# The remainders of one weight slot in four move from VectorE to GpSimd

## The reference

```
mod = silu(c) @ w_mod + b_mod                          # 2048 -> 6 x 2048
proj = (rmsnorm(x, pre_mix_g) * (1 + scale_a) + shift_a) @ w_in
q = rmsnorm(q_lat) @ w_uq ;  kv = rmsnorm(kv_lat) @ w_ukv
x = x + gate_a * rmsnorm(concat(attn, hgrn) @ w_out)
x = x + gate_m * rmsnorm(square(relu(h @ w_up)) @ w_down)
proj = rmsnorm(x) @ w_in_2
merged = sigmoid(ga) * (att @ w_attn_o) + sigmoid(gb) * (silu(ln(conv)) @ w_conv_o)
x = x + rmsnorm(merged @ w_out_2)
x = x + rmsnorm((silu(gate) * up) @ w_down_2)
```

## Time and profile before

| | |
|---|---|
| median of 3 runs | 2996.82 us (2993.32 to 3002.66) |
| profiled execution | 2995.96 us, span 2994.2 us |
| TensorE (PE) busy | 2751.9 us, 92% |
| VectorE (DVE) busy | 1968.1 us, 66% |
| ScalarE (ACT) busy | 1201.4 us, 40% |
| GpSimd (POOL) busy | 22.6 us, 1% |
| w_lo, VectorE, full chunks | 852 x 1223 ns |

### The profile page before, as it was taken

How to read it: one execution, slowest core, us unless ns; L and a number is a source line. 1 busy time by engine, 2 the same in 40 slices (tenths; PEclk the granted TensorE clock), 3 DMA queues, 4 the chain that set the end, 5 groups by cost and what they waited for, 6 DMA issues and landing times.

```text
span 2994.2 us, 41611 instructions
## 1 busy us (share of the span) xinstructions
PE 2751.9 (92%) x14939; PEld 2350.7 (79%) x14939; DVE 1968.1 (66%) x2489; ACT 1201.4 (40%) x1521; POOL 22.6 (1%) x42
## 2 busy tenths in 40 slices
PE   2299898699799999999979999999979999999998
PEld 2288797567688888888868878887768888888886
DVE  6899685569888445664464878867565565565444
ACT  2134323334444334444344434454444444444433
POOL 1000000000000000000010000000000000000000
PEclk7599899789899999999989999999989999999999
DMA  9799432329487556665546555555536666656554
GB/s 320 254 366 367 150 113 55 108 77 324 155 282 261 177 189 185 188 184 186 179 131 185 176 171 153 164 163 164 171 96 191 184 183 188 188 182 204 182 184 147
DMA packets 491558, 563.46 MB, mean 188 GB/s; under 512 B 17943, under 2 KB 434131, under 8 KB 491072
## 3 DMA queue, kind: packets, MB, share of 16 engines
q1 hardware_dynamic: 489824, 558.18, 58.4%
q0 software_dynamic: 1632, 3.89, 0.6%
HBM read 559.90 MB, written 2.10 MB: 188 GB/s over the span
## 4 chain that ended last, share of the span: by engine, by line
PE 78%; DVE 10%; DMA 8%; ACT 2%; issue 2%; DVEq 0%; SPq 0%; ACTq 0%
PE ps L653 42%; PE ps L655 21%; DMA w_raw<-in_w_in 5%; PE ps L688 3%; PE ps L689 3%; PE ps L690 3%; DMA w_raw<-in_w_mod 2%; PE ps L843 2%; DVE w_lo L1265 2%; DVE mod_acc L1307 2%; ACT w_hi L996 1%; DVE mod_acc_a L1541 1%; PE ps L793 1%; PE ps L720 1%; DVE rstd L1385 1%
## 5 line engine op out<-in xcount | busy, mean ns | idle before, releaser
L653 PE MATMUL ps<-acts,w_hi 128*128 128x512 f32 x4976 | 1780.8, 402 | 46.0 <-DVE acts L1403 15.5
L1265 DVE TENSOR_TENSOR w_lo<-w_raw,w_hi 128x1024 fp32r<-128x1024 f32 (+1 forms) x872 | 1055.1, 1213 | 737.6 <-ACT w_hi L996 601.3
L655 PE MATMUL ps<-acts,w_lo 128*128 128x256 f32 x4976 | 1400.7, 281 | 0.0
L996 ACT CAST w_hi<-w_raw 128x1024 fp32r<-128x1024 f32 (+1 forms) x784 | 814.5, 1042 | 1198.5 <-PE ps L655 1044.5
L653 PEld LDWEIGHTS ps<-acts,w_hi 128*128 128x128 f32 x4976 | 941.3, 189 | 288.3 <-issue 45.6
L655 PEld LDWEIGHTS ps<-acts,w_lo 128*128 128x128 f32 x4976 | 946.5, 190 | 2.1 <-issue 1.7
L653 PE MATMUL ps<-ff,w_hi 128*128 128x512 f32 x1024 | 361.7, 397 | 0.0
L655 PE MATMUL ps<-ff,w_lo 128*128 128x256 f32 x1024 | 288.4, 282 | 0.0
L653 PEld LDWEIGHTS ps<-ff,w_hi 128*128 128x128 f32 x1024 | 193.4, 189 | 45.5
L1307 DVE SCALAR_TENSOR_TENSOR mod_acc<-mod_w,silu_c,mod_acc 128x512 f32<-128x512 f32 (+1 forms) x300 | 192.8, 643 | 9.4 <-DVE mod_acc L1307 0.6
L655 PEld LDWEIGHTS ps<-ff,w_lo 128*128 128x128 f32 x1024 | 193.9, 189 | 0.1
(11 more groups left out here) (244 smaller groups left out, 1612.8 us busy)
## 6 DMA issues: line engine op xcount, KB each, us to landing
w_raw<-in_w_in SPq DMA_DIRECT2D x236, 512.0 KB, 4.4
w_raw<-in_w_down SPq DMA_DIRECT2D x216, 512.0 KB, 3.5
w_raw<-in_w_gate_up SPq DMA_DIRECT2D x176, 512.0 KB, 3.6
mod_w<-in_w_mod SPq DMA_DIRECT2D x128, 512.0 KB, 8.3
w_raw<-in_w_up SPq DMA_DIRECT2D x128, 512.0 KB, 4.1
w_raw<-in_w_mod SPq DMA_DIRECT2D x64, 512.0 KB, 5.2
w_raw<-in_w_out SPq DMA_DIRECT2D x64, 512.0 KB, 4.8
w_raw<-in_w_attn_o SPq DMA_DIRECT2D x16, 512.0 KB, 3.4
```

What stands on the lines that cost most here:

```text
L653: pe.matmul(ps[:, bank, :], hi, lin_.act[:, kk, :, :], start=at_first, stop=False, skip_group_check=True)
L655: mm = pe.matmul(ps[:, bank, 0:T], lo, lin_.act[:, kk, 0, :], start=False, stop=at_last, skip_group_check=True)
L996: act.copy(w_hi[:, slot, 0:kn, 0:lin_.width], w_raw[:, slot, 0:kn, 0:lin_.width]).then_inc(hi_ready, 1)
L1265: dve.tensor_tensor(low[cut], raw[cut], high[cut].bitcast(F32), ALU.subtract).then_inc(lo_ready, 1)
```

## The change

GpSimd computes the remainder of the chunks in slot 3, VectorE those of slots 0 to 2. `lo_ready` becomes four counters, one per slot, and `lo_uses` gives the count that a chunk's remainder brings its slot to. SP and TensorE wait for the counter of the chunk's own slot. VectorE no longer waits for `hi_ready` of slot 3 and goes on to what stands beside the chunk. GpSimd's remainders stand in its queue around the DMAs it already issued.

```diff
-        lo_ready = sem("lo_ready")
+        lo_ready = [sem(f"lo_ready{s}") for s in range(SLOTS)]
...
+        def lo_uses(ph, it, j):
+            return ph.use0[j % SLOTS] + it * ph.slot_uses[j % SLOTS] + (j // SLOTS + 1 - DT)
...
-                    sp.wait_ge(lo_ready, free)
+                    sp.wait_ge(lo_ready[j % SLOTS], lo_uses(ph, it, j) - 1)
...
+            def remainders(ph, it):
+                slot = SLOTS - 1
+                for j in range(slot, ph.n_chunks, SLOTS):
+                    b, _, kn = ph.chunks[j]
+                    lin_ = ph.body[b][0]
+                    cut = (slice(None), slot, slice(0, kn), slice(0, lin_.width))
+                    raw, high, low = wide if lin_.by_token else (w_raw, w_hi, w_lo)
+                    pool.wait_ge(hi_ready, chunk_seq(ph, it, j) + 1)
+                    pool.tensor_tensor(low[cut], raw[cut], high[cut].bitcast(F32),
+                                       ALU.subtract).then_inc(lo_ready[slot], 1)
...
+            remainders_of(("in_h", "in_m"))
             pool.wait_ge(h_lo, 1)
             pool.dma_start(pos_i[ROPE:P, :],
...
+            remainders_of(("uq", "ukv", "w_o", "up_0", "down_0", "up_1", "down_1"))
             pool.wait_ge(*r_m1.added(4))
...
                     pool.dma_start(bias[rows, r // 2, :, i, :], src).then_inc(bias_landed, 16)
+            remainders_of(("in_c", "in_qk", "in_v", "in_g", "att_o", "conv_o", "out_2", "gate_up"))
             pool.wait_ge(extra, extra_all("gate_up"))
             pool.dma_start(g_row[:, :], ...
+            remainders_of(("down_2",))
...
-                    pe.wait_ge(lo_ready, chunk_seq(ph, it, j) + 1)
+                    pe.wait_ge(lo_ready[slot], lo_uses(ph, it, j))
...
-                    dve.wait_ge(hi_ready, chunk_seq(ph, it, j) + 1)
-                    (the subtraction into w_lo)
+                    if slot < SLOTS - 1:
+                        dve.wait_ge(hi_ready, chunk_seq(ph, it, j) + 1)
+                        (the subtraction into w_lo, which signals lo_ready[slot])
```

More of the change, by code:

```diff
@@ L612, in _, with remainders_of @@
                 pool.dma_start(dst, src).then_inc(late_loads, 16)
+            def remainders(ph, it):
[8 more added lines that the diff above has]
+                                       ALU.subtract).then_inc(lo_ready[slot], 1)
+            def remainders_of(names):
+                for ph in phases:
+                    if ph.name in names:
+                        remainders(ph, 0)
+                        if ph.iters > 1:
+                            with pool.Fori(1, ph.iters) as it:
+                                remainders(ph, it)
+            remainders_of(("in_h", "in_m"))
             pool.wait_ge(h_lo, 1)
@@ L678, in token_panel @@
                     slot = j % SLOTS
-                    pe.wait_ge(lo_ready, chunk_seq(ph, 0, j) + 1)
+                    pe.wait_ge(lo_ready[slot], lo_uses(ph, 0, j))
                     if b == 0 and ph.name in ready:
@@ L1261, in split @@
                     kn, slot = ph.chunks[j][2], j % SLOTS
-                    dve.wait_ge(hi_ready, chunk_seq(ph, it, j) + 1)
[L1263 to L1266, removed]
+                    if slot < SLOTS - 1:
+                        dve.wait_ge(hi_ready, chunk_seq(ph, it, j) + 1)
+                        cut = (slice(None), slot, slice(0, kn), slice(0, lin_.width))
+                        raw, high, low = wide if lin_.by_token else (w_raw, w_hi, w_lo)
+                        dve.tensor_tensor(low[cut], raw[cut], high[cut].bitcast(F32),
+                                          ALU.subtract).then_inc(lo_ready[slot], 1)
                     if not (first and b == 0):
```

## The result

| | before | after |
|---|---|---|
| median of 5 runs | 2993.32 us (2988.75 to 3002.66) | 3019.46 us (3010.91 to 3023.06) |
| ratio after / before | | 1.0082, 95% interval [1.0057, 1.0108] |
| profiled execution (span) | 2995.96 (2994.2) | 3010.91 (3009.1) |

The change makes the kernel slower by 0.8%: 24.5 us by the ratio (the medians differ by 26.1), against 22.5 forecast.

A forecast was written before the change was run, and what follows sets the result against it. TensorE was taken to bound most stages, with VectorE not spare in in_h (beside DMA) and w_o. Terms 12 + 5.5 + 1 + 1 + 1 + 2 = 22.5 us on 2995.96 gave 3018 us, forecast's own range 3006 to 3036.

The forecast's parts named there:

- ring argument: Slot ring, all panels: reload ends 8 to 9 us into the 11.3 us slot period, hiding the longer remainder.
- L: Length of GpSimd's new subtraction: taken as 2.4 us, twice VectorE's row, bounded by 1.22 and 7.0 us.
- The standing still: VectorE stops while GpSimd's subtraction reads SBUF, for instructions with two SBUF operands: 1.8 to 2.4 us each.
- The net per panel: VectorE time per panel: 1.8 to 2.4 us added for 1.14 removed, net +0.66 to +1.26 us.
- w_o: Stage at 665 to 740 us, VectorE back to back: about 6 panels, 4 to 8 us lost, 5.5 taken.
- in_h: Stage at 146 to 320 us: 15 panels, each 0.5 to 1.1 us over the DMA's 11.45; 12 us taken.
- stage ends: POOL's new queue order and evictions where stages end: -2 to +5 us together, 2 taken.
- Rival A: VectorE is not stopped: w_o panels fall to 12.15 us, total 2985 to 2991 us; chance 0.28.
- B: Rival: L is 3 to 5 us and VectorE is stopped; about 3058 us at 3.4; chance 0.12.
- C: Rival: L over 6 us, GpSimd paces every panel; 3170 us at 7.0; chance 0.04.
- D: Rival: the stop falls into idle time or is shared, half of L charged; near 2998 us; chance 0.08.
- The break-even: VectorE per panel: a partial stop costs as much as the relief gives at 1.14 us, 48% of L.

The follow-up runs named there:

- e5: Kernel before with 22 unused GpSimd subtractions added beside it, 15 in in_h and 7 in w_o, nothing moved; 3020.28 us, ratio to before 1.0088.
- e2: Changed kernel, but GpSimd subtracts only one column of slot 3's remainders (very first chunk whole), the rest left out; 2983.5 us, ratio to before 0.9969.
- e4: Changed kernel, but GpSimd computes slot 3 only in in_h and w_o; 3011.88 us, ratio to before 1.0063.
- e3: Changed kernel, but VectorE computes all four remainders in in_h and w_o; 3001.31 us, ratio to before 1.0031.
- e1: Changed kernel with its four counters, but VectorE computes all four remainders; 2992.17 us, ratio to before 1.0001.
- e6: Changed kernel, but GpSimd subtracts only the first half of each slot 3 chunk, the rest left out; 2987.31 us, ratio to before 0.9999.

## Why the prediction was right

**The place.** Both stages that it named carry the loss, and down_0 to down_1 are untouched at full TensorE, as the ring argument said.

**L.** 2.4 us taken, 2.49 measured (mean of the full chunks); at the end, where nothing disturbs it, 2.39 to 2.40. The rows of before only bounded it between 1.22 and 7.0, so the value was a choice and not a measurement, and it met the mark.

**The standing still.** Taken on the word of a rule, since no row of before showed it. Now rows do: the lengthened instructions of after, the unstopped one with a PSUM operand (691 against 685 ns), e5 where nothing was moved, and e2 where it is gone. The prediction's condition, two operands from SBUF, is too narrow: L1333 with one is stopped as well. The Trainium skill (SBUF — State Buffer, "SBUF: two separate sides") states the exclusion for the whole instruction; by that, the trace agrees for a stop caught in full (2.2 of 2.49 us). On the mean a subtraction cost 1.6 us of VectorE's recorded durations in e5 (22 of them, 35 us), 1.9 in e4, and 2.1 us of a panel of w_o (after against e2), where the prediction had 1.8 to 2.4.

**The net per panel.** +0.66 to +1.26 forecast. w_o: +1.10. in_h: +0.69 over its transfers, where 0.5 to 1.1 was forecast.

**in_h**, 12 us: about 10 (14 to 15 panels at 0.69); 11.7 is what the table has with in_m and the attention in it. **w_o**, 5.5 us: 7.7. The step that was mis-sized is the count: the prediction took about 6 panels, and the stage has seven to eight; the price per panel was inside its bounds. That in_h came out some 2 us under and w_o some 2 over is why the sum of the two fits so well, and that is luck.

**up_0**, 1 us: 0, by the cover it named, idle VectorE time. **in_qk and the start of in_c**, 1 us and a share of the stage ends: 2.7. The stop in the apply of in_c was named at up to 2.4 us and was 4.3. VectorE, then GpSimd, where in_c begins in after:

```profile
1570.00 0.42 DVE L1429 TENSOR_TENSOR acts<-ring,acts 128x256 fp32r<-128x256 f32 x1
1570.34 4.80 DVE L1440 SCALAR_TENSOR_TENSOR ring<-x_res,cols,rstd 128x256 f32<-128x256 f32 x1
1575.06 0.41 DVE L1429 TENSOR_TENSOR acts<-ring,acts 128x256 fp32r<-128x256 f32 x1
```
```profile
1561.62 10.84 POOL L652 DMA_DIRECT2D bias<-in_rpb  x16 [28.77 <-DVE x_res L1453]
1572.46 2.39 POOL L627 TENSOR_TENSOR w_lo<-w_raw,w_hi 128x1024 fp32r<-128x1024 f32 x1
```

**in_v, in_g**, 1 us: 1.7; **att_o to out_2**, part of the stage ends: 2.0. The sum of these small terms, with up_0, was 5 forecast and is 6.2 by the landmarks; e3 puts them at 0.31%, 9 us. Which it is, one profile can't say, with TensorE's pace wandering by 2% in stretches. It stays open.

**The counters**, 0: 0 (e1). **Rival A** is refuted by its own number: w_o at 12.15 was its mark, and only e2 comes there. B and C fall with L; D would have charged half of L, 1.2 us, and 1.9 to 2.1 is charged (e4; w_o). One sign of the prediction did not show: TensorE's longer waits for w_lo are named by VectorE (47.8 us) and hardly by GpSimd (4.6), since the remainder that comes late is the stopped engine's own. **The break-even** at a charge of 1.14 us is borne out by e6.

## What to carry to other kernels

Work given to GpSimd is not free for VectorE when both work on SBUF: count the helper's duration against the work taken away. Here 2.4 us given for 1.14 taken loses in both stages where VectorE has next to no idle time (in_h, w_o); at 1.33 us the exchange is even; and in up_0, where VectorE had 1.0 us of idle time a panel, it costs nothing. Look for the stop in the durations of VectorE's instructions, not in its waits. Where an engine paces a stage, first look for fixed cost in its own short instructions (749 ns against 2 x 483).

## What the runs showed of the hardware

- One VectorE instruction of 0.48 us took 4.80 where in_c begins (above). The stop of 4.3 us is longer than the GpSimd subtraction's recorded 2.39 and begins up to 2.1 us before it, while 16 DMA issues of the same engine were ending. In before the same issues lay beside the same apply and did not slow it. The excess goes with the length of the subtraction: in e6, with half of it, two instructions take 1.49 us there, the first of them (from 1552.37) over before the subtraction's recorded start (1554.49), and in e2, with one element, none is longer than 0.49. What holds VectorE before the recorded start was not isolated.
- GpSimd's recorded duration grows too, from 2.39 to 3.49 us (200.92 in in_h), when VectorE runs a subtraction of its own at that moment (200.93 to 202.15): the waiting goes both ways.
- GpSimd's subtraction by length: 222 ns for one element a partition, 1278 for 512, 1828 for 768, 2.4 us for 1024: about 0.2 us and 2.1 ns an element, where VectorE's takes 1223 ns for 1024.
- TensorE runs one and the same code at two paces, 567 to 569 or 578 to 579 matmuls in 100 us, at a granted clock of 1.00, in stretches that change within an execution and do not follow the kernel. Its cause stays open.
- The first attention took very different times in single executions. Between the last eviction of uq and the first of w_o lie 110.4 us in before and 111.8 in after, at a granted clock of 0.78 and 0.80, but 127.1 in e2 and 130.3 in e5, at 0.64 and 0.66. e5's edit puts next to nothing into this stretch, and after, with every remainder of slot 3 on GpSimd, does not show it. So 15 to 20 us, nearly what the change costs, can come or go there in one profiled execution, whose cause stays open: one more reason to read panels and the ratio of many executions and not one span.
